# The low halves of weight units, and four sums of squares, computed on VectorE instead of GpSimd in a two-block transformer kernel

## The reference

```python
# first block: x is [512, 1024]
h = rmsnorm(x, norm_ffn_g)
u = causal_dwconv(h @ w_up, conv_w, conv_b)      # three taps along the tokens
gate, val = jnp.split(u, 2, axis=-1)             # 2816 each
x = x + (jax.nn.silu(gate) * val) @ w_down
x = rmsnorm(x, norm_final_g)
# second block
x = x + 0.5 * rms_norm(swiglu(rms_norm(x, g1), w_gate, w_up, w_down), g2)
#   sparse attention, a gated linear recurrence and a merge of both:
#   proj2, branch (two gated products, added), out
x = x + rms_norm(merged @ w_out, g3)
x = x + 0.5 * rms_norm(swiglu(...), g4)
#   a last projection with a gate (ple)
```

## Time and profile before

| | |
|---|---|
| time, median of 3 runs (lowest to highest) | 2147.24 us (2144.21 to 2147.51) |
| span of the profiled execution | 2145.4 us |
| mean granted clock of TensorE | 0.950 |
| PE busy | 1915.8 us, 89% |
| DVE busy | 1164.5 us, 54% |
| ACT busy | 653.4 us, 30% |
| POOL busy | 820.7 us, 38% |
| chain that ended last | PE 68%, DVE 21%, issue 6%, POOL 2% |

### The profile page before, as it was taken

The page is one execution under the profiler, slowest core; times in us unless marked ns, Lnnn a source line. Parts: engine busy times, 40 slices in busy tenths (PEclk is TensorE's granted clock), DMA queues, the critical chain, the costliest instruction groups (busy, mean ns, idle before and its releaser), DMA issues.

```text
span 2145.4 us, 23938 instructions
## 1 busy us (share of the span) xinstructions
PE 1915.8 (89%) x8290; PEld 1507.0 (70%) x8290; DVE 1164.5 (54%) x1521; ACT 653.4 (30%) x968; POOL 820.7 (38%) x397
## 2 busy tenths in 40 slices
PE   5999888888879899999979998977888799999986
PEld 4666676666658688888856777666656588888864
DVE  6345548888820454443253477767674654442246
ACT  4333321111212322222233333543443322222243
POOL 2121233333434454444443334433234454444441
PEclk9898899999989899999989999999989899999988
DMA  3111122222212132223212233231132123233212
GB/s 129 57 63 52 56 73 84 78 78 78 92 60 94 47 111 98 96 95 106 94 60 89 74 113 113 70 123 45 55 123 88 59 98 97 93 105 114 90 40 79
DMA packets 55461, 180.63 MB, mean 84 GB/s; under 512 B 6336, under 2 KB 7104, under 8 KB 55392
## 3 DMA queue, kind: packets, MB, share of 16 engines
q1 hardware_dynamic: 43200, 157.07, 22.0%
q10 hardware_dynamic: 12192, 22.67, 3.1%
HBM read 167.65 MB, written 12.06 MB: 84 GB/s over the span
## 4 chain that ended last, share of the span: by engine, by line
PE 68%; DVE 21%; issue 6%; ACT 2%; POOL 2%; DMA 1%; DVEq 1%; ACTq 0%; SPq 0%; POOLq 0%
PE bank L716 16%; PE bank L717 16%; PE bank L718 16%; DVE val L1851 3%; DVE val L1849 3%; PE bank L738 2%; PE bank L740 2%; PE bank L739 2%; PE bank L797 2%; PE bank L799 2%; PE bank L798 2%; DVE sq L1844 1%; POOL w_lo L604 1%; DVE a_lo L1617 1%; DVE chunk L1666 1%
## 5 line engine op out<-in xcount | busy, mean ns | idle before, releaser
L604 POOL TENSOR_TENSOR w_lo<-raw,w_hi 128x1024 fp32r<-128x1024 f32 (+2 forms) x273 | 703.9, 2585 | 1122.1 <-ACT w_hi L1110 1122.1
L716 PE MATMUL bank<-a_hi,w_hi 128*128 128x512 f32 x1312 | 520.9, 397 | 40.8 <-POOL w_lo L604 20.3
L1110 ACT ACTIVATE w_hi<-raw 128x1024 fp32r<-128x1024 f32 (+2 forms) x281 | 302.4, 1086 | 764.5 <-PE bank L718 697.5
L717 PE MATMUL bank<-a_lo,w_hi 128*128 128x512 f32 x1312 | 512.2, 390 | 0.0
L718 PE MATMUL bank<-a_hi,w_lo 128*128 128x512 f32 x1312 | 512.1, 390 | 0.0
L716 PEld LDWEIGHTS bank<-a_hi,w_hi 128*128 128x128 f32 x1312 | 247.0, 188 | 120.9 <-issue 45.9
L718 PEld LDWEIGHTS bank<-a_hi,w_lo 128*128 128x128 f32 x1312 | 247.2, 188 | 52.5
L717 PEld LDWEIGHTS bank<-a_lo,w_hi 128*128 128x128 f32 x1312 | 247.2, 188 | 49.7 <-issue 0.8
L716 PE MATMUL bank<-h_hi,w_hi 128*128 128x512 f32 x568 | 222.0, 391 | 20.1 <-DVE h_lo L1860 17.6
L717 PE MATMUL bank<-h_lo,w_hi 128*128 128x512 f32 x568 | 221.7, 390 | 0.0
L718 PE MATMUL bank<-h_hi,w_lo 128*128 128x512 f32 x568 | 221.5, 390 | 0.0
(11 more groups left out here) (261 smaller groups left out, 2418.0 us busy)
## 6 DMA issues: line engine op xcount, KB each, us to landing
raw<-in_w_up SPq DMA_DIRECT2D x132, 512.0 KB, 3.4
raw<-in_w_down SPq DMA_DIRECT2D x48, 704.0 KB, 4.1
raw<-in_w_proj SPq DMA_DIRECT2D x59, 512.0 KB, 3.5
raw<-in_w_wo SPq DMA_DIRECT2D x8, 512.0 KB, 3.4
raw<-in_w_branch SPq DMA_DIRECT2D x16, 256.0 KB, 2.7
gates_in<-spill ACTq DMA_DIRECT2D x16, 256.0 KB, 3.3
raw<-in_w_out SPq DMA_DIRECT2D x8, 512.0 KB, 3.8
raw<-in_w_ple SPq DMA_DIRECT2D x8, 512.0 KB, 3.4
```

The source lines that it names most:

```text
L604: pool.tensor_tensor(lo, src, hi.bitcast(F32), ALU.subtract).then_inc(unit_split, 1)
L716: mm(dst[:, :], wh, hi[:, k, :], start=(first and c == 0), stop=False)
L717: mm(dst[:, :], wh, lo[:, k, :], start=False, stop=False)
L1110: fn(w_hi[:, slot, 0:size], raw[:, slot, 0:size], ACT.Copy).then_inc(unit_high, 1)
```

## The change

The work of GpSimd on weight units ends with the first four units of wo; after that GpSimd only makes the low halves of 34 units of proj2, from unit 4 on (as before), the masks of the sparse attention and the differences of the recurrence. Everywhere else VectorE makes them, with a new `split_unit`, at places written out by hand. That is 219 units: 158 of 128x1024, 48 of 128x1408, 13 of 128x512. The 28 additions of `add_squares` go to VectorE too, as four copies and 28 additions (`add_square`). ScalarE makes the high half of the third unit of the next stage already before the last tile of a stage is finished (`last_tile_finished`), and that of unit 3 after the fourth chunk of `scaled_highs` instead of before the first. The loops over pairs are cut: the first and the last pair of tiles stand outside of the loop. No matmul is added or removed.

```diff
@@ GpSimd @@
-            for name, n, _ in STAGES[:6]:
-                split_units(name, 0, min(n, SLOTS))
-                if name in POOL_SUMS:
-                    add_squares(POOL_SUMS[name])
-                split_units(name, SLOTS, n)
-            split_units("proj2", 0, SLOTS)
-            add_squares("mixpre")
+            split_units("proj1", 0, UNIT["proj1"][1])
+            split_units("wo", 0, SLOTS)
+            pool.wait_ge(unit_split, UNIT["proj2"][0] + SLOTS)
             split_units("proj2", SLOTS, LEAD2 + 3)
...
-            pool.wait_ge(unit_split, UNIT["branch"][0] + 3)
-            split_units("branch", 3, 2 * DC)
-            for name, n, _ in STAGES[8:]:
-                split_units(name, 0, min(n, SLOTS))
-                if name in POOL_SUMS:
-                    add_squares(POOL_SUMS[name])
-                split_units(name, SLOTS, n)
@@ ScalarE @@
+            def last_tile_finished(stage):
+
+                v = UNIT[stage][0] + UNIT[stage][1]
+                if stage.startswith("down"):
+                    units_done(v - 1)
+                unit_high_part(v + 2)
+                act.wait_ge(unit_done, v)
...
             def scaled_highs(stage, g, before, units):
 
-                unit_high_part(UNIT[units][0] + 3)
                 for k in range(DC):
                     act.wait_ge(x_ready, before + k + 1)
                     scaled_high(g, k)
                     square(stage, k, x[:, k, :], (x_ready, before + k + 1))
+                    if k == 3:
+                        unit_high_part(UNIT[units][0] + 3)
@@ VectorE @@
+            def split_unit(u, it=0, per_loop=0):
+
+                slot, size = u % SLOTS, BLOCKS_OF[u] * P
+                dve.wait_ge(unit_high, u + 1 + it * per_loop)
+                v.tensor_tensor(w_lo[:, slot, 0:size], raw[:, slot, 0:size], w_hi[:, slot, 0:size].bitcast(F32),
+                                ALU.subtract).then_inc(unit_split, 1)
...
-            def scaled_done(stage):
+            def scaled_done(stage, units):
 
                 dve.sem_inc(chunk_ready, DC)
+                split_unit(UNIT[units][0] + 3)
                 rsqrt(stage)
...
+            def splits_after(stage, k):
+
+                u = UNIT[stage][0]
+                if stage.startswith("down"):
+                    if k < DC - 1:
+                        split_unit(u + 2 * k + 3)
+                        split_unit(u + 2 * k + 4)
+                elif 0 < k < DC - 1:
+                    split_unit(u + k + 3)
+
+            def late_splits(stage, k):
+
+                u = UNIT[stage][0]
+                if stage.startswith("down") and k == DC - 2:
+                    split_unit(u + 2 * DC + 1)
+                    split_unit(u + 2 * DC + 2)
+                if not stage.startswith("down") and k == DC - 1:
+                    split_unit(u + DC + 2)
...
                     if k and split:
                         scaled_low(split[0], split[1], k - 1)
+                        add_square(split[0], k - 1)
...
+            def conv_pairs(turn, it=0, skip=0):
...
-                        dve.wait_ge(tile_sem("up1", i), TILE["up1", i][1] + 1 + it)
+                        dve.wait_ge(tile_sem("up1", i), TILE["up1", i][1] + 1 + turn + it)
+                        if i >= skip:
+                            split_unit(first + 4 * turn + i + 3, it, 4)
...
+            conv_pairs(0, skip=1)
+            at_loop = steps[0]
+            with dve.Fori(0, FC // 2 - 2) as it:
+                conv_pairs(1, it)
...
+            conv_pairs(FC // 2 - 1)
...
                         v.tensor_tensor(slots[j][:, :], bank[g][:, :], rstd[:, :], ALU.mult).then_inc(bank_free[g], 1)
-                        dve.wait_ge(unit_done, first + 2 * j + 2 + it * 4)
+                        if 2 * j >= skip:
+                            split_unit(u0 + 2 * j + 3, it, 4)
+                        dve.wait_ge(unit_done, u0 + 2 * j + 2 + it * 4)
...
-                        dve.wait_ge(hidden_ready, FC * turn + j + 1 + it * 2)
+                        dve.wait_ge(hidden_ready, n + it * 2)
+                        split_unit(u0 + 2 * j + 4, it, 4)
...
             def branch_kept(stage, square_stage):
                 for k in range(DC):
+                    wait(tile_done(stage, k))
+                    splits_after(stage, k)
                     add_square(square_stage, k)
+                    late_splits(stage, k)
...
                 low(c, h_lo[:, m, :], h_hi[:, m, :])
+                for u in (2 * m + 3, 2 * m + 4) if m else (4,):
+                    split_unit(UNIT["branch"][0] + u)
+            split_unit(UNIT["out"][0] + 3)
```

More of the change, by code:

```diff
@@ L99 @@
 EARLY = {UNIT[name][0] + 3 for name in ("proj1", "wo", "up1", "up2", "proj2", "branch", "out", "up3", "ple")}
-POOL_SUMS = {"up2": "pre1", "proj2": "mixpre", "up3": "pre2", "ple": "plepre"}
 BLOCKS_OF = [c for _, n, c in STAGES for _i in range(n)]
@@ L1894, in hiddens @@
+                        v.tensor_tensor(hidden_at(h_lo, it, 2 * at + j), val[:, :],
+                                        hidden_at(h_hi, it, 2 * at + j).bitcast(F32), ALU.subtract).then_inc(
                             hidden_ready, 1)
-                        dve.wait_ge(hidden_ready, FC * turn + j + 1 + it * 2)
-                steps[0] += 2 * (FC // 2 - 1)
+                        dve.wait_ge(hidden_ready, n + it * 2)
+                        split_unit(u0 + 2 * j + 4, it, 4)
+                pairs(0, skip=1)
@@ L1898, in branch_kept @@
+                with dve.Fori(0, FC // 2 - 2) as it:
+                    pairs(1, it)
+                steps[0] += 2 * (FC // 2 - 3)
+                pairs(FC // 2 - 1)
             def branch_kept(stage, square_stage):
                 for k in range(DC):
+                    wait(tile_done(stage, k))
+                    splits_after(stage, k)
                     add_square(square_stage, k)
+                    late_splits(stage, k)
             hiddens("up2", 1)
@@ L1906, in _ @@
             dve.sem_inc(chunk_ready, DC)
+            split_unit(UNIT["proj2"][0] + 3)
             invert("mixpre")
@@ L2109, in _ @@
                     act_ready, 1)
+            split_unit(UNIT["branch"][0] + 3)
             dve.wait_ge(hg_loaded, 16 * HEADS)
```

86 lines of the change are left out of this document (43 added, 43 removed).

## The result

The changed kernel took **2093.86 us** (median of 4 runs, 2091.62 to 2099.14), the kernel before 2147.38 beside it; the ratio is 0.9762 with a 95% interval of 0.9744 to 0.978.

What follows compares the result with a forecast made beforehand. VectorE, stalled by GpSimd's work, was taken to pace up1, TensorE up2. 2145.4 - 38.9 - 10.8 + 6.4 + 1.8 + 2 = 2105.9, plus 1.8 from span to median: 2108 us, range 2098 to 2124.

Steps and rivals of the forecast that it cites:

- 22 x (13.29 - 11.52) = 38.9 us less: Up1: each of 22 pairs of tiles falls from 13.29 to 11.52 us, VectorE still pacing; 38.9 us less.
- the 9.02: Up1: VectorE's time for a pair without GpSimd beside it, 9.02 us, before two low halves add 2.50.
- Sum 10.8 less: Stage ends and starts: shorter additions of squares, chunks and low-half waits together save 10.8 us.
- I count only 0.4 in each of proj2, up3 and ple: Starts of proj2, up3 and ple: chunks 2.66 us apart against 3.05 save 0.4 each, 1.2 in all.
- bound of 1.14: Up1: lowest price in us of a low half on VectorE, giving 11.30 a pair and 43.8 less.
- the overlap of 0.08: VectorE at up2's start: a read begins 0.08 us before the previous one ends; basis of the lowest low-half price.
- Up2 and up3, 6.4 more: Up2 and up3: unit 4's low half stands behind the first pair, costing 3.2 us in each stage.
- for TensorE's clock: New gaps in branch and at unit 4 may lower TensorE's granted clock; 2 us added.
- Branch, 1.8 more: Branch: longer periods of 6.8 us and a later unit 4, less shorter waits at end and beginning; 1.8 us more.
- Slower: Up1: something other than GpSimd, such as weight-load traffic, makes taps long and stays; 2209 us, chance 3%.
- No gain: Up1: dead time behind each low half, or worst coupling to the high half, makes a pair 13.4; 2149 us, 5%.
- Larger gain: Up1: waits hide part of a low half, so TensorE paces at 10.87 a pair; 2087 to 2098 us, 5%.

Runs made afterwards that it cites:

- the busy GpSimd: The changed kernel with 80 unneeded subtractions of 128x1024 on GpSimd, begun after up1's fourth unit; 2195.93 us, ratio 1.0248.
- the three-turn loop: The changed kernel with three turns (six pairs) in each pass of VectorE's up1 loop, register waits kept; 2088.29 us, ratio 0.9726.

## Why the prediction missed its range

Its direction and its mechanism were right. Two terms of the sum were too small, up1 by 8 us and the stage ends by 12; terms that were too small on the other side (unit 4, branch) and proj2, longer for a reason that no run shows, hid about 9 of it.

- **Up1, the step "22 x (13.29 - 11.52) = 38.9 us less".** From up1's first matmul to the wait at its end the first traces give 316.1 and 269.0, 47.1 less (46.6 in the second traces). Where the missing 8.2 are:
  - The pairs in the loop. A low half was priced at 1.25; there it starts 0.82 after the read and the tap 1.14 after it, where the tap started 0.89 after the read before: it adds 1.07. Against that, the loop's end, 0.6 in every second pair, was missing in the 9.02. Together a loop pair takes 11.40 instead of 11.52, only 1.4 more than forecast in all.
  - The second pair, which the change writes out, takes 10.06: 1.5 more.
  - The first pair was counted like the others. Before the change it took 12.4 from its first read to `h_lo` (312.41 to 324.81), now 8.2: 2.4 more.
  - The last three distances were 13.87, 14.88 and 11.67 before, since low halves of 1408 ran beside them, and are 11.09, 10.63 and 10.86 now: 2.5 more.
  - The rest, 0.3, is the earlier start. The pairs outside the loop escape the register waits, and the forecast priced all 22 by a pair inside it.
- **Stage ends, the step "Sum 10.8 less".** They gave 22.6, in the means of the traces: wo 3.5, down1 1.4, the way to `pre1` 0.9, down2 2.6, the way to `mixpre` 5.6, out 3.0, and 2.8 each to `pre2` and `plepre`. What failed is "I count only 0.4 in each of proj2, up3 and ple". The rhythm of the chunks was forecast right, 2.66 against 3.05; the rows below are starts of chunks in the kernel after, and the kernel before has 3.01 to 3.10 between them. But five distances of a stage have it, so that first and last chunk lie 1.75 closer together (18.79 to 17.04), and the way from the last chunk to the sum, where GpSimd's last addition lengthened VectorE's chain, is 1.0 shorter: 2.8 instead of 0.4. With the squares alone put back, 2.8, 2.7 and 2.1 of the gain on the three ways to `mixpre`, `pre2` and `plepre` are gone.

```profile
1056.34 0.74 DVE L1685 SCALAR_TENSOR_TENSOR chunk<-y,par,rstd 128x512 f32<-128x512 f32 x1
...
1059.00 0.74 DVE L1685 SCALAR_TENSOR_TENSOR chunk<-y,par,rstd 128x512 f32<-128x512 f32 x1
```

- **The range was too narrow.** The bound of 1.14 for a low half, from the overlap of 0.08, gave 43.8 us; the 1.07 and the 47.1 lie beyond both. With that bound the sum is 2102.8, and the range ended 5 us below it, with all other terms at their middles.
- **Up2 and up3, 6.4 more**: the two gaps are there (2.65 each, `w_lo` the releaser), but with the lower clock behind them they cost 4.3 to 5.8 each, 10.2 in the mean of the traces. The 2 us "for TensorE's clock" are half of the difference.
- **Branch, 1.8 more**, was too little: from its first product to out's first matmul it is 4.6 more. The wait at its end became shorter as forecast (8.58 to 5.51), but the period is 7.06 instead of 6.8, and, counted from that product, TensorE is done with branch 7.6 later than before.
- **Proj2 and what follows up to branch, forecast at nothing,** is 4.3 longer (441.3 from `mixpre` to branch's first product in both traces before, 445.0 and 446.2 after). In the eight other traces of kernels built on the changed one it is 440.4 to 443.6, in two kernels built on the kernel before 440.7 and 444.0, so that most of it looks like variation; no run was made to show it.
- **The rivals.** "Slower" falls by the busy GpSimd: the stalls are GpSimd's. "No gain" needed a dead time behind each low half; the flush that the Trainium skill's *VectorE: DVE Perf Modes* ("The DRAIN you can't avoid") describes does not show: the tap starts 1.14 to 1.15 us after a low half of 1.22. (The same section adds, which the prediction left out, that an operation that is not held starts earlier.) "Larger gain" asked for a pair at TensorE's pace, 10.87; the pair was 11.26, and that needed one more edit, the loop written out. That the measured 2093.9 lies within this rival's 2087 to 2098 is luck: the missing us came from the edges of up1 and from the stage ends.

## What to carry to other kernels

Don't weigh an offload to GpSimd by GpSimd's own time: where VectorE is the bound, a subtraction of 128x1024 on GpSimd cost VectorE 2.0 us here and the same subtraction on VectorE 1.1, and moving it back in up1 paid 46 of 53.5 us. Count the stalls of the small operations too: at the stage ends, where they were nearly left out, 22.6 us were gained instead of 10.8. When a term is n times a pair, look at the first and the last pairs by themselves, and at whether the edit takes them out of the loop; 6 of the missing 8 us of up1 were there. After work is moved onto an engine, look for the one place in each stage where it stands behind something long (unit 4, branch): placing the low halves of these two in the engine's waits gave another 18 us.

## What the runs showed of the hardware that was not expected

- VectorE and GpSimd take turns by whole instructions: beside a GpSimd that never pauses, each of VectorE's operations of 512 columns from SBUF to SBUF takes 2.0 to 2.3 us from start to start, whether it lasts 0.43 or 0.75 alone, with one tensor input as with two; reads of a PSUM bank stay at 0.69.
- On VectorE a loop whose waits and addresses are register values costs 1.0 us for a pair of 13 operations, and 0.6 to 0.7 at its end. With VectorE's up1 loop written out the times fell by 18 us (kernel after) and 30 us (kernel before). The Trainium skill, in *Runtime: NRT & Kernel Launch* ("Instruction fetch mechanics"), names a taken branch whose target is not at hand as a cost and says that kernels prefer full unrolling for it; the three-turn loop shows that here the loop's end is the smaller part, 0.3 of 1.3 us a pair. Whether the target was at hand no run shows.
- A gap of 2.65 us on TensorE cost 4.3 to 5.8, the rest at a granted clock of 0.50 behind it.
